# Where the input matrices of a state space are formed: on the states' partitions, or on the channels' partitions

## The chip, the cores and the metric

The kernel runs on one core of a Trainium2 chip. The metric is device time in microseconds (us), the median of several executions. It was 3431.4 us in 3 runs of the kernel before (3431.08 to 3432.77).

## The reference

The model is a stack of four layers on 512 tokens of width 2048, all in float32. The first layer holds gated linear attention (GLA) and forgetting attention, the second a diagonal state space (S5), and the last two other mixtures. Only the state space matters here:

```python
# 128 groups of 16 channels, each with a 64-dim complex diagonal state
step = exp(log_step); mag = exp(lr * step)
lb = mag * (cos(li * step) + 1j * sin(li * step))      # the power of one token
coef = (lb - 1) / (lr + 1j * li)
bb = coef[..., None] * b                                # scaled B: state x channel
x_t = lb * x_{t-1} + bb @ u_t
y_t = real(c @ x_t) + d * u_t
```

The kernel works it in blocks of `ST` = 8 tokens. For a block it needs, for each pair of groups, a matrix that takes 8 tokens of 16 channels (128 rows, token e and channel c) to the 128 states of the pair. Its entry is the scaled B of the channel times the power 7 - e of lb. These "B tables" do not depend on x, so they are made early and stored in DRAM.

## The kernel before

**Products and helpers.** Nearly all time goes to weight products (line 631). Each float32 product is made of three passes of rounded halves. A weight piece of 512 KB is loaded by SP into a ring of 4 (`load_piece`, line 351), ACT makes its high half (line 390), DVE the low half (line 396), PE then multiplies: 24 matmuls of 512 columns for a usual piece. SP issues the load of piece n+7, ACT and DVE split piece n+3, and PE multiplies piece n, all at the same place of their programs. `load_piece` waits until DVE has split the piece that held the slot.

**Side work.** Each engine runs a generator of side steps woven among its pieces by `beside` and `between` (line 855). For the first phase, `GLA_IN` (41 pieces), the side work is `prep_*` (lines 2061 to 2353). It has 56 steps: a lead of 4, then 8 slices (`SSL`) of 6 steps, called `at` 0 to 5, and 4 last ones. A slice is 8 pairs of groups. About four pieces, 8 half pieces, lie in a slice. No engine keeps time with another except through semaphores; an instruction that waits holds up all that stands behind it on its engine, the pieces too.

**Steps of a slice before.** DVE scales B (`scaled_b`, `at` 0, six instructions of 128 elements), multiplies it by the eight powers (`b_powers`, `at` 1 and 2, twice three instructions of 1024 elements, lines 2292 to 2294) and does the same for C (`c_powers`, `at` 3 and 4, lines 2304 to 2309), then the phases (`at` 5). PE turns the B tables by 16 transposes (`turn_b`, `at` 2 and 3, line 2119), and turns C by 4 (line 2109, `at` 5). In `at` 0 of the next slice it makes 32 small products (`kernels`, line 2130), which need `c_powers` of the slice done. ACT copies the turned B from PSUM to `s_BT` (four copies of 512 columns, line 2170), among other copies. SP stores the phases' table (`s_turns`, `at` 1), loads the next slice's B and C (12 DMAs, lines 2070 and 2075, `at` 2), stores the small products of the slice before (`s_k`, 8 DMAs, line 2096, `at` 3), and stores `s_bt` and `s_c_powers` (line 2078, `at` 5). Slice 0 has no `s_k`.

After the phase POOL waits for all tables and loads the operands of GLA (`gla_pool`, line 969).

Of the kernel before, what the change touches and what calls it, by code (L numbers as in the profile page):

```python
# [127 lines left out]
def build(nc, inp, out):  # L128
# [840 lines left out]
    def gla_pool(pool):  # L969
        wait_stored(pool, GLA_IN)  # L970
        pool.wait_ge(s5_kept, 16 * PREP_TABLES * SSL)
        pool.wait_ge(s5_kept_k, 16 * SPAIR * SSL)
# [1009 lines left out]
    def diff_first(pool):  # L1982
# [34 lines left out]
    V5 = overlay(HALF, [  # L2017
        ("s_b", [2, SPAIR, SC], F32), ("s_B", [2, SPAIR, SC], F32), ("s_BP", [2, SPAIR, 2, SC], F32), ("s_cn", [4, P], F32),
        ("s_c", [2, SPAIR, SC], F32), ("s_C", [2, SPAIR, E9, SC], F32), ("s_tp", [SPAIR, E9, SC], F32),
        ("s_L", [2, SPAIR, ST, SC], F32), ("s_t", [SPAIR, ST, SC], F32), ("s_BT", [2, SPAIR, P], F32), ("s_cs", [3, SPAIR, SK], F32),  # L2020
        ("s_n", [SPAIR, SK], F32), ("s_K", [2, 2 * P], F32), ("s_d", [NPAIR // 4, SC], F32),
        ("s_same", [4 * SC], F32)])
    V6 = overlay(0, [
# [25 lines left out]
    PREP_LOADS, PREP_TABLES = 12, 3  # L2049

    def s5_natural(n):

# [8 lines left out]
    def prep_sp(sp):  # L2061
# [15 lines left out]
        def keep(table, n, sl):  # L2077
            sp.dma_start(table[sl], n).then_inc(s5_kept, 16)

        for step, sl, at in prep_slots():  # L2080
            if step == 0:
                sp.wait_ge(x_stored, 16)
# [10 lines left out]
            if at == 3 and 0 < sl <= SSL:  # L2093
                sp.wait_ge(s5_k, sl)
                for n in range(SPAIR):
                    sp.dma_start(k_dram[sl - 1][:, n, :, :], V5["s_K"][n * SC:(n + 1) * SC, :, :]).then_inc(s5_kept_k, 16)
            if at == 5 and 0 <= sl < SSL:
                sp.wait_ge(s5_bte, 2 * sl + 2)
                keep(bt_dram, V5["s_BT"][:, :, :, :].rearrange("p n j x -> p (n j x)"), sl)
                sp.wait_ge(s5_c, sl + 1)  # L2100
                keep(c_dram, V5["s_C"][:, :, :, :, :].rearrange("p n j e c -> p (n j e c)"), sl)
            yield

    def prep_pe(pe):
        def turn_c(sl):
            pe.wait_ge(s5_in, 16 * PREP_LOADS * (sl + 1))
            pe.wait_ge(s5_bte, 2 * sl)
# [4 lines left out]
        def turn_b(sl, n):  # L2112
            pe.wait_ge(s5_l, 2 * sl + n + 1)
            if n == 0:
                pe.wait_ge(s5_cc, sl + 1)
            else:
                pe.wait_ge(s5_ke, sl)
            for j in range(SPAIR):
                ins = nc.tensor.transpose(pm[2 * n + j // 4][:, j % 4 * P:(j % 4 + 1) * P], V5["s_L"][:, n, j, :, :], ident[:, :])
            ins.then_inc(s5_bt, 1)  # L2120

        def kernels(sl):
            pe.wait_ge(s5_bte, 2 * sl + 2)
            pe.wait_ge(s5_c, sl + 1)
            pe.wait_ge(s5_bp, sl + 1)
            for half_of in range(2):
# [8 lines left out]
        for step, sl, at in prep_slots():  # L2135
            if at == 0 and 0 < sl <= SSL:
                kernels(sl - 1)
            if at in (2, 3) and 0 <= sl < SSL:
                turn_b(sl, at - 2)
            if at == 5 and sl < SSL - 1:  # L2140
                turn_c(sl + 1)
            yield
# [1 line left out]
    def prep_act(act):  # L2144
# [21 lines left out]
        def copy_b(sl, n):  # L2166
            act.wait_ge(s5_bt, 2 * sl + n + 1)
            act.wait_ge(s5_kept, 16 * PREP_TABLES * sl)
            for h in range(2):
                ins = nc.scalar.activation(V5["s_BT"][:, n, 4 * h:4 * h + 4, :], pm[2 * n + h][:, :], ACT.Copy)  # L2170
                run(ins) if h == 0 else ins.then_inc(s5_bte, 1)
# [13 lines left out]
        for step, sl, at in prep_slots():  # L2185
# [18 lines left out]
                copy_kernels(sl - 1)  # L2204
            if at == 1 and 0 <= sl < SSL:
                spread_b(sl)
            if at in (3, 4) and 0 <= sl < SSL:
                copy_b(sl, at - 3)
            yield

    def prep_dve(dve):
# [57 lines left out]
        def scaled_b(sl):  # L2269
# [4 lines left out]
            dve.wait_ge(s5_l, 2 * sl)  # L2274
            for n in range(2):
                run(tt(t[:, :, 0, :], V5["s_b"][:, n, :, :], over_c(S_CR), ALU.mult))
                run(tt(t[:, :, 1, :], V5["s_b"][:, 1 - n, :, :], over_c(S_CI), ALU.mult))
# [1 line left out]
                run(ins) if n == 0 else ins.then_inc(s5_b, 1)  # L2279

        def b_powers(sl, n):
            js = slice(sl * SPAIR, (sl + 1) * SPAIR)
            power = lambda c: ang[:, c, :ST, js].rearrange("p e j -> p j e").unsqueeze(3).broadcast_to([P, SPAIR, ST, SC])
            b3 = lambda x: V5["s_B"][:, x, :, :].unsqueeze(2).broadcast_to([P, SPAIR, ST, SC])
            if n == 0:
                dve.wait_ge(s5_b, sl + 1)
                dve.wait_ge(s5_sc, 3)
            else:
                dve.wait_ge(s5_l, 2 * sl + 1)
            if sl:  # L2290
                dve.wait_ge(s5_bt, 2 * (sl - 1) + n + 1)
            run(tt(V5["s_L"][:, n, :, :, :], b3(n), power(0), ALU.mult))
            run(tt(t[:, :, :, :], b3(1 - n), power(1), ALU.mult))
            tt(V5["s_L"][:, n, :, :, :], V5["s_L"][:, n, :, :, :], t[:, :, :, :], ALU.subtract if n == 0 else ALU.add).then_inc(s5_l, 1)

        def c_powers(sl, n):
            js = slice(sl * SPAIR, (sl + 1) * SPAIR)
# [24 lines left out]
        for step, sl, at in prep_slots():  # L2322
# [22 lines left out]

    def prep_pool(pool):
# [12 lines left out]
    def s5_sp(sp):  # L2359
# [40 lines left out]
    def s5_pe(pe):  # L2400
        for sl in range(SSL):
# [4 lines left out]
            ins.then_inc(s5_ut, 1)  # L2406
            yield
            pe.wait_ge(s5_ute, sl + 1)
            pe.wait_ge(s5_bt_in, 16 * (sl + 1))
            pe.wait_ge(s5_ze, 2 * sl)  # L2410
            for n in range(2):
                for g in range(NG):
# [71 lines left out]
    def s5_dve(dve):  # L2484
# [353 lines left out]
```

## Time and profile before

| | |
|---|---|
| median of 3 runs | 3431.4 us |
| profiled execution | 3432.28 us |
| its span | 3430.5 us |
| PE busy in the span | 3341.5 us (97%) |
| DVE busy | 1638.5 us (48%) |
| ACT busy | 1291.4 us (38%) |
| mean granted clock | 0.991 |
| share of 16 DMA engines of the main hardware queue | 33.0% |

The span is counted from the first to the last instruction. The clock is that which TensorE was granted, as a part of full speed. Busy shares are means over stages of different make; the stage that the change touches lies between about 57 and 310 us. SP computes nothing, so the table has no row for it: its time is that of issuing DMAs and of waiting.

### The profile page before, as it was taken

The numbers are of one execution on the slowest core, as the hardware profiler recorded it, in microseconds if no ns is written. First come the engines' busy times: TensorE is split into PE (matmuls) and PEld (weight loads), VectorE is DVE, ScalarE is ACT, GpSimd is POOL, SyncE is SP. The second block draws the span as 40 slices with busy tenths as digits, with TensorE's granted clock in tenths as the row PEclk, the third lists the DMA queues.
The fourth block names the chain that finished last, engine by engine and source line by source line (L and its number), as shares of the span: only waits on it lengthen the run. The fifth ranks groups of instructions, "written<-read, shape, count | busy, mean of one in ns | idle before, by whom it ended". The sixth has DMA issues, their size and how long they took to land.

```text
span 3430.5 us, 41764 instructions
## 1 busy us (share of the span) xinstructions
PE 3341.5 (97%) x16431; PEld 2700.0 (79%) x16431; DVE 1638.5 (48%) x2695; ACT 1291.4 (38%) x2000; POOL 515.0 (15%) x749
## 2 busy tenths in 40 slices
PE   7999999999999999999999899999999999999998
PEld 6777887887888888888888676788878888777886
DVE  7895655344343454444343556553424343355443
ACT  4443433343233333433342436532323323355432
POOL 0001312322110000110330011021000111110211
PEclk9999999999999999999999999999999999999999
DMA  6776433546348776544335343363433643433642
GB/s 211 216 231 199 132 105 105 154 145 208 132 160 227 210 215 184 173 159 141 123 111 170 119 129 102 122 214 119 147 88 111 200 151 117 132 111 102 208 148 92
DMA packets 279523, 525.06 MB, mean 153 GB/s; under 512 B 64189, under 2 KB 99588, under 8 KB 274720
## 3 DMA queue, kind: packets, MB, share of 16 engines
q1 hardware_dynamic: 223504, 340.79, 33.0%
q0 software_dynamic: 53648, 178.32, 15.2%
q10 hardware_dynamic: 2176, 3.28, 0.4%
q8 instruction: 131, 2.15, 0.3%
q14 instruction: 64, 0.52, 0.0%
HBM read 408.32 MB, written 113.97 MB: 152 GB/s over the span
## 4 chain that ended last, share of the span: by engine, by line
PE 73%; DVE 3%; ACT 3%; issue 2%; DMA 1%; POOL 0%; ACTq 0%; POOLq 0%; DVEq 0%
PE pg L631 64%; PE pm L1322 2%; PE pm L1351 2%; PE pm L1338 1%; PE pm L2426 1%; ACT whi L390 1%; DMA mx_g<-zt 1%; PE pm L2430 0%; PE pm L2414 0%; DVE r_y L1707 0%; DVE d_x L2514 0%; PE pm L2405 0%; ACT stage L501 0%; PE pm L1819 0%; ACT w_p L1387 0%
## 5 line engine op out<-in xcount | busy, mean ns | idle before, releaser
L396 DVE TENSOR_TENSOR wlo<-raw,whi 128x1024 fp32r<-128x1024 f32 x523 | 663.2, 1273 | 1251.5 <-ACT whi L390 1250.5
L390 ACT ACTIVATE whi<-raw 128x1024 fp32r<-128x1024 f32 x523 | 548.7, 1054 | 1100.3 <-PE pg L631 1090.2
L631 PE MATMUL pg<-a_hi,whi 128*128 128x512 f32 x1856 | 743.9, 401 | 11.4 <-DVE wlo L396 4.8
L631 PE MATMUL pg<-a_hi,wlo 128*128 128x512 f32 x1856 | 726.7, 392 | 0.0
L631 PE MATMUL pg<-a_lo,whi 128*128 128x512 f32 x1856 | 726.2, 391 | 0.0
L631 PE MATMUL pg<-b_hi,whi 128*128 128x512 f32 x1568 | 620.8, 396 | 8.7 <-DVE stage L572 3.2
L631 PE MATMUL pg<-b_hi,wlo 128*128 128x512 f32 x1568 | 612.2, 390 | 0.0
L631 PE MATMUL pg<-b_lo,whi 128*128 128x512 f32 x1568 | 611.5, 390 | 0.0
L631 PEld LDWEIGHTS pg<-a_hi,whi 128*128 128x128 f32 x1856 | 348.4, 188 | 90.7 <-issue 14.2
L631 PEld LDWEIGHTS pg<-a_hi,wlo 128*128 128x128 f32 x1856 | 348.1, 188 | 77.5
L631 PEld LDWEIGHTS pg<-a_lo,whi 128*128 128x128 f32 x1856 | 348.7, 188 | 73.6 <-issue 2.6
L631 PEld LDWEIGHTS pg<-b_hi,whi 128*128 128x128 f32 x1568 | 295.3, 188 | 73.9 <-issue 6.4
L631 PEld LDWEIGHTS pg<-b_hi,wlo 128*128 128x128 f32 x1568 | 294.9, 188 | 62.5
L631 PEld LDWEIGHTS pg<-b_lo,whi 128*128 128x128 f32 x1568 | 295.3, 188 | 60.8 <-issue 1.2
L673 POOL DMA_DIRECT2D zt<-stage x144 | 78.1, 545 | 569.6 <-DVE stage L572 290.3
L631 PE MATMUL pg<-whi,a_hi 128*128 128x512 f32 x384 | 156.5, 407 | 0.0
L631 PE MATMUL pg<-wlo,a_hi 128*128 128x512 f32 x384 | 150.8, 393 | 0.0
L631 PE MATMUL pg<-whi,a_lo 128*128 128x512 f32 x384 | 150.4, 392 | 0.0
L1387 ACT ACTIVATE m_p<-m_p,m_small 128x128 f32<-128x128 f32 (+3 forms) x96 | 54.1, 563 | 211.0 <-DVE m_small L1453 210.6
L1450 DVE CUSTOM_DVE_ANT_0 m_p<-pm,wide 128x128 f32<-128x128 f32 (+3 forms) x96 | 47.1, 491 | 138.7 <-PE pm L1322 69.5
L685 POOL TENSOR_TENSOR acc<-acc,xa_sq 128x512 f32<-128x512 f32 x44 | 60.9, 1384 | 314.0 <-ACT xa_sq L525 309.1
L631 PE MATMUL pg<-whi,b_hi 128*128 128x512 f32 x256 | 101.7, 397 | 0.0
(442 smaller groups left out, 3843.7 us busy)
## 6 DMA issues: line engine op xcount, KB each, us to landing
raw<-in_l_w_in SPq DMA_DIRECT2D x169, 512.0 KB, 3.7
raw<-in_ab_w_in SPq DMA_DIRECT2D x112, 512.0 KB, 3.7
zt<-stage POOLq DMA_DIRECT2D x142, 256.0 KB, 3.6
raw<-in_c_w_in SPq DMA_DIRECT2D x64, 512.0 KB, 4.9
raw<-in_l_w_out SPq DMA_DIRECT2D x64, 512.0 KB, 3.9
raw<-in_ab_w_out SPq DMA_DIRECT2D x32, 512.0 KB, 3.8
raw<-in_glu_w SPq DMA_DIRECT2D x32, 512.0 KB, 4.2
raw<-in_c_w_out SPq DMA_DIRECT2D x32, 512.0 KB, 3.7
```

The source lines that it names most:

```text
L390: nc.scalar.activation(used(whi, n), used(raw, n), ACT.Copy).then_inc(hi_ready, 1)
L396: nc.vector.tensor_tensor(used(wlo, n), used(raw, n), used(whi, n).bitcast(F32), ALU.subtract).then_inc(lo_ready, 1)
L631: ins = nc.tensor.matmul(pg[m][:r.rows(m), :r.cols()], lhsT, rhs, start=(kt == 0 and n_pass == 0), stop=(kt == r.kts - 1 and n_pass == 2))
L673: pool.dma_start(r.dst(i, m, r), stage[:r.rows(m), m, :r.cols()]).then_inc(stored[m], 16)
L685: nc.gpsimd.tensor_tensor(total[:, :], total[:, :], squares[:, m % 2, :], ALU.add).then_inc(acc_done, 1)
L1322: ins = nc.tensor.matmul(pm[n % 2][:, :count * P], lhsT, rhs, start=(i == 0), stop=(i == len(ops) - 1))
L1338: ins = nc.tensor.transpose(pm[2][:, at:at + P], p[:, b * P:(b + 1) * P], ident[:, :])
L1351: ins = nc.tensor.matmul(pm[3][o * a.dv:(o + 1) * a.dv, qb * P:(qb + 1) * P], a.value(t, o, first + b), a.buf["pt"][:, n % 2, at:at + P], ...
L1387: nc.scalar.activation(p, p, ACT.Exp, bias=a.buf["small"][:, s:s + 1], accum_out=a.buf["small"][:, 4 + s:5 + s]).then_inc(att["probs"], 1)
L1450: run(vec.tensor_tensor_reduce(out=a.buf["p"][:, s, :count * P], in0=pm[n % 2][:, :count * P], in1=a.bias(t, qb, count), scale=a.scale, sc ...
L2426: nc.tensor.matmul(y_of(j), V6["d_x"][:, n, j, :, :].rearrange("p g k -> p (g k)"), V6["d_C"][:, n, j, 1:, :], start=(n == 0 and j % 4 == ...
```

## The change

B tables are now formed with (token, channel) on the partitions. The powers are turned once, by 8 transposes (`turn_powers`), copied by ACT and stored in DRAM as rows. For each slice the scaled B is turned by 2 transposes, copied by one ACT instruction and stored in DRAM (`b_rows`). When this store has landed, SP issues 24 loads (`repeat_rows`), each into 16 partitions, which repeat the rows of B for the eight tokens and each power row for the 16 channels. DVE multiplies the two in the following slice (`b_powers(sl - 1)`, still six instructions of 1024 elements), straight into `s_BT`, and SP stores the table one slice later, too. Semaphores of the later state-space phase are used twice, so its counts are offset.

```diff
+        def repeat_rows(sl):
+            for e in range(ST):
+                rows_of = slice(e * SC, (e + 1) * SC)
+                power = powers_rows[:, e:e + 1, sl * SPAIR:(sl + 1) * SPAIR, :].rearrange("n a j x -> a n (j x)")
+                sp.dma_start(V5["s_Pr"][rows_of, :, :, :].rearrange("p n j x -> p n (j x)"),
+                             power.broadcast_to([SC, 2, SPAIR * P])).then_inc(rows_repeated, 16)
+                for n in range(2):
+                    sp.dma_start(V5["s_Br"][rows_of, n, :, :], b_rows[sl][:, n, :].rearrange("(j c) x -> c j x", c=SC)).then_inc(
+                        rows_repeated, 16)
...
+            if at == 0 and sl == 0:
+                sp.wait_ge(s5_bte, 1)
+                sp.dma_start(powers_rows.rearrange("n (h e) j x -> (e j) (n h) x", e=2), V5["s_BT"][:, 0, :, :]).then_inc(rows_kept, 16)
+            if at == 3 and 0 < sl <= SSL:
+                sp.wait_ge(s5_l, 2 * sl)
+                sp.dma_start(bt_dram[sl - 1], V5["s_BT"][:, :, :, :].rearrange("p n j x -> p (n j x)")).then_inc(b_tables_kept, 16)
+            if at == 3 and 0 <= sl < SSL:
+                sp.wait_ge(s5_bte, sl + 2)
+                sp.dma_start(b_rows[sl], V5["s_bT"][:, :, :]).then_inc(rows_kept, 16)
+            if at == 4 and 0 <= sl < SSL:
+                sp.wait_ge(rows_kept, 16 * (sl + 2))
+                repeat_rows(sl)
             if at == 5 and 0 <= sl < SSL:
-                sp.wait_ge(s5_bte, 2 * sl + 2)
-                keep(bt_dram, V5["s_BT"][:, :, :, :].rearrange("p n j x -> p (n j x)"), sl)
                 sp.wait_ge(s5_c, sl + 1)
                 keep(c_dram, V5["s_C"][:, :, :, :, :].rearrange("p n j e c -> p (n j e c)"), sl)
...
-            for j in range(SPAIR):
-                ins = nc.tensor.transpose(pm[2 * n + j // 4][:, j % 4 * P:(j % 4 + 1) * P], V5["s_L"][:, n, j, :, :], ident[:, :])
+        def turn_powers():
+            pe.wait_ge(s5_sc, 3)
+            for n in range(2):
+                for h in range(ST // 2):
+                    ins = nc.tensor.transpose(pm[1 + 2 * n][:, h * P:(h + 1) * P],
+                                              T5["s_ang"][:, n, 2 * h:2 * h + 2, :].rearrange("p e j -> p (e j)"), ident[:, :])
             ins.then_inc(s5_bt, 1)
+        def turn_b(sl):
+            pe.wait_ge(s5_b, sl + 1)
+            pe.wait_ge(s5_bte, sl + 1)
+            for n in range(2):
+                ins = nc.tensor.transpose(pm[3][:, n * P:(n + 1) * P], V5["s_B"][:, n, :, :].rearrange("p j c -> p (j c)"), ident[:, :])
+            ins.then_inc(s5_bt, 1)
...
+        def copy_b(sl):
+            act.wait_ge(s5_bt, sl + 2)
+            act.wait_ge(rows_kept, 16 * (sl + 1))
+            nc.scalar.activation(V5["s_bT"][:, :, :], pm[3][:, :2 * P], ACT.Copy).then_inc(s5_bte, 1)
...
         def b_powers(sl, n):
...
             if n == 0:
+                dve.wait_ge(rows_repeated, 16 * ROW_LOADS * (sl + 1))
+                dve.wait_ge(rows_kept, 16)
+                dve.wait_ge(b_tables_kept, 16 * sl)
+            to, by, tp = V5["s_BT"][:, n, :, :], V5["s_Pr"], t.rearrange("p j e c -> p j (e c)")
+            run(tt(to, V5["s_Br"][:, n, :, :], by[:, 0, :, :], ALU.mult))
+            run(tt(tp, V5["s_Br"][:, 1 - n, :, :], by[:, 1, :, :], ALU.mult))
+            tt(to, to, tp, ALU.subtract if n == 0 else ALU.add).then_inc(s5_l, 1)
...
-                if at in (1, 2):
-                    b_powers(sl, at - 1)
...
+            if at in (1, 2) and 0 < sl <= SSL:
+                b_powers(sl - 1, at - 1)
```

## Rows read from the trace of the kernel before

**Rows 1.** Windows: length, busy time of each engine, PEclk, DMA share, GB/s.

```profile
80.00:300.00 220.00, 214.28 (x1224) 169.06 (x1223) 190.19 (x215) 92.48 (x156) 15.68 (x25) 1.00 0.74 228
50.00:55.00 5.00, 2.96 (x7) 2.39 (x8) 4.75 (x5) 3.57 (x4) 0.00 (x0) 0.52 0.37 93
```

**Rows 2.** Waits of PE, DVE and SP between 80 and 300 us: total, times, longest.

```profile
PE pm L2119 <- DVE s_L L2294: 5.7, 8, 1.0
...
DVE wlo L396 <- ACT whi L390: 24.5, 13, 6.1
...
SPq L369 <- DVE wlo L396: 79.9, 22, 11.0
SPq L2078 <- DVE s_C L2309: 22.6, 8, 3.1
```

**Rows 3.** Timeline of SP: start, time and count of merged issues; slice 1 to 2.

```profile
126.08 0.47 SPq L2078 DMA_DIRECT2D s_bt<-s_BT  x1
129.23 0.33 SPq L2078 DMA_DIRECT2D s_c_powers<-s_C  x1
132.75 4.75 SPq L369 DMA_DIRECT2D raw<-in_ab_w_in  x2
137.54 1.38 SPq L2078 DMA_DIRECT2D s_turns<-s_cs  x1
...
147.03 0.50 SPq L369 DMA_DIRECT2D raw<-in_ab_w_in  x1
147.57 3.87 SPq L2096 DMA_DIRECT2D s_k<-s_K  x8
151.51 0.40 SPq L369 DMA_DIRECT2D raw<-in_ab_w_in  x1
151.96 0.47 SPq L2078 DMA_DIRECT2D s_bt<-s_BT  x1
```

**Rows 4.** SP's timeline at slice 0's store, and in the later state-space phase.

```profile
99.73 0.46 SPq L2078 DMA_DIRECT2D s_bt<-s_BT  x1
...
1088.27 6.23 SPq L2373 DMA_DIRECT2D d_MG<-s_k  x8
```

**Rows 5.** DMA issues: count, KB each, median us to landing; the last from 1050 to 1350 us.

```profile
s_bt<-s_BT SPq DMA_DIRECT2D x8, 1024.0 KB, 6.4
...
s_k<-s_K SPq DMA_DIRECT2D x64, 32.0 KB, 3.0
s_cn<-in_s_c_re SPq DMA_DIRECT2D x32, 32.0 KB, 1.9
...
d_MG<-s_k SPq DMA_DIRECT2D x64, 128.0 KB, 8.6
```

**Rows 6.** Timeline of DVE in slice 7: first b_powers, its end, and last c_powers.

```profile
269.18 1.28 DVE L2292 TENSOR_TENSOR s_L<-s_B,s_ang 128x1024 f32<-128x1024 f32 x1
...
275.53 1.23 DVE L2294 TENSOR_TENSOR s_L<-s_L,s_t 128x1024 f32<-128x1024 f32 x1
276.68 1.22 DVE L396 TENSOR_TENSOR wlo<-raw,whi 128x1024 fp32r<-128x1024 f32 x1
...
285.91 1.36 DVE L2309 SCALAR_TENSOR_TENSOR s_C<-s_C,s_tp 128x1152 f32<-128x1152 f32 x1
```

**Rows 7.** Timeline of PE at the first eight transposes of a slice, and at `turn_c`.

```profile
219.03 0.39 PE L631 MATMUL pg<-wlo,a_hi 128*128 128x512 f32 x1
220.17 1.10 PE L2119 MATMUL pm<-ident,s_L 128*128 128x128 f32 x8 [0.74 <-DVE s_L L2294]
221.02 0.48 PE L631 MATMUL pg<-whi,a_hi 128*128 128x512 f32 x1
...
232.86 0.40 PE L631 MATMUL pg<-wlo,a_hi 128*128 128x512 f32 x1
233.09 0.60 PE L2109 MATMUL pm<-ident,s_cn 128*128 128x128 f32 x4
233.45 0.47 PE L631 MATMUL pg<-whi,a_hi 128*128 128x512 f32 x1
```

**Rows 8.** Timeline: the last `kernels` on PE, POOL's first GLA load, its user.

```profile
288.77 1.08 PE L2130 MATMUL pm<-s_C,s_BP 128*32 128x128 f32 x32
...
308.70 0.52 POOL L973 DMA_DIRECT2D g_lr<-zt  x1 [3.56 <-DMA zn<-stage]
...
325.36 1.12 PE L1023 MATMUL pm<-g_lr,g_up 16*128 16x512 f32 x2
```

More of the change, by code:

```diff
@@ L971, in gla_pool @@
         pool.wait_ge(s5_kept, 16 * PREP_TABLES * SSL)
+        pool.wait_ge(b_tables_kept, BEFORE_BT)
         pool.wait_ge(s5_kept_k, 16 * SPAIR * SSL)
@@ L2019, in build @@
         ("s_c", [2, SPAIR, SC], F32), ("s_C", [2, SPAIR, E9, SC], F32), ("s_tp", [SPAIR, E9, SC], F32),
-        ("s_L", [2, SPAIR, ST, SC], F32), ("s_t", [SPAIR, ST, SC], F32), ("s_BT", [2, SPAIR, P], F32), ("s_cs", [3, SPAIR, SK], F32),
+        ("s_Br", [2, SPAIR, P], F32), ("s_Pr", [2, SPAIR, P], F32), ("s_bT", [2, P], F32), ("s_t", [SPAIR, ST, SC], F32), ("s_BT", [2, SPAIR, P], F32), ("s_cs", [3, SPAIR, SK], F32),
         ("s_n", [SPAIR, SK], F32), ("s_K", [2, 2 * P], F32), ("s_d", [NPAIR // 4, SC], F32),
@@ L2028, in build @@
     bt_dram, c_dram = dram("s5_bt", (SSL, P, 2 * SPAIR * P)), dram("s5_c_powers", (SSL, P, 2 * SPAIR * E9 * SC))
+    b_rows, powers_rows = dram("s5_b_rows", (SSL, P, 2, P)), dram("s5_powers_rows", (2, ST, NPAIR, P))
     cs_dram, k_dram = dram("s5_turns", (SSL, P, 3 * SPAIR * SK)), dram("s5_k", (SSL, SC, SPAIR, 2, 2 * P))
@@ L2048, in build @@
     PREP_STEPS = PREP_LEAD + PREP_SLOT * SSL + PREP_LAST
-    PREP_LOADS, PREP_TABLES = 12, 3
+    PREP_LOADS, PREP_TABLES = 12, 2
+    ROW_LOADS = 3 * ST
+    b_tables_kept, rows_kept, rows_repeated = s5_bt_in, s5_cs_in, s5_mat_in
+    BEFORE_BT, BEFORE_CS, BEFORE_MAT = 16 * SSL, 16 * (SSL + 1), 16 * ROW_LOADS * SSL
     def s5_natural(n):
@@ L2106, in turn_c @@
             pe.wait_ge(s5_in, 16 * PREP_LOADS * (sl + 1))
-            pe.wait_ge(s5_bte, 2 * sl)
+            pe.wait_ge(s5_cc, sl)
             for i in range(4):
@@ L2110, in turn_c @@
             ins.then_inc(s5_ct, 1)
[L2112 to L2117, printed above, removed]
-            for j in range(SPAIR):
-                ins = nc.tensor.transpose(pm[2 * n + j // 4][:, j % 4 * P:(j % 4 + 1) * P], V5["s_L"][:, n, j, :, :], ident[:, :])
+        def turn_powers():
[10 more added lines that the diff above has]
+                ins = nc.tensor.transpose(pm[3][:, n * P:(n + 1) * P], V5["s_B"][:, n, :, :].rearrange("p j c -> p (j c)"), ident[:, :])
             ins.then_inc(s5_bt, 1)
         def kernels(sl):
-            pe.wait_ge(s5_bte, 2 * sl + 2)
+            pe.wait_ge(s5_ke, sl)
             pe.wait_ge(s5_c, sl + 1)
@@ L2137, in prep_pe @@
                 kernels(sl - 1)
-            if at in (2, 3) and 0 <= sl < SSL:
-                turn_b(sl, at - 2)
+            if at == 0 and sl == 0:
+                turn_powers()
+            if at == 1 and 0 <= sl < SSL:
+                turn_b(sl)
             if at == 5 and sl < SSL - 1:
@@ L2164, in copy_c, with copy_powers @@
                     run(ins) if n + g < 2 else ins.then_inc(s5_cc, 1)
[L2166 to L2171, printed above, removed]
+        def copy_powers():
+            act.wait_ge(s5_bt, 1)
+            for n in range(2):
+                ins = nc.scalar.activation(V5["s_BT"][:, 0, 4 * n:4 * n + 4, :], pm[1 + 2 * n][:, :], ACT.Copy)
+                run(ins) if n == 0 else ins.then_inc(s5_bte, 1)
+        def copy_b(sl):
+            act.wait_ge(s5_bt, sl + 2)
+            act.wait_ge(rows_kept, 16 * (sl + 1))
+            nc.scalar.activation(V5["s_bT"][:, :, :], pm[3][:, :2 * P], ACT.Copy).then_inc(s5_bte, 1)
         def phase_sines(sl):
@@ L2206, in prep_act @@
                 spread_b(sl)
-            if at in (3, 4) and 0 <= sl < SSL:
-                copy_b(sl, at - 3)
+            if at == 0 and sl == 0:
+                copy_powers()
+            if at == 2 and 0 <= sl < SSL:
+                copy_b(sl)
             yield
@@ L2273, in scaled_b @@
             dve.wait_ge(s5_bp, sl)
-            dve.wait_ge(s5_l, 2 * sl)
+            dve.wait_ge(s5_bt, sl + 1)
             for n in range(2):
@@ L2281, in b_powers @@
         def b_powers(sl, n):
-            js = slice(sl * SPAIR, (sl + 1) * SPAIR)
-            power = lambda c: ang[:, c, :ST, js].rearrange("p e j -> p j e").unsqueeze(3).broadcast_to([P, SPAIR, ST, SC])
-            b3 = lambda x: V5["s_B"][:, x, :, :].unsqueeze(2).broadcast_to([P, SPAIR, ST, SC])
             if n == 0:
-                dve.wait_ge(s5_b, sl + 1)
-                dve.wait_ge(s5_sc, 3)
-            else:
-                dve.wait_ge(s5_l, 2 * sl + 1)
[L2290 to L2294, printed above, removed]
+                dve.wait_ge(rows_repeated, 16 * ROW_LOADS * (sl + 1))
[5 more added lines that the diff above has]
+            tt(to, to, tp, ALU.subtract if n == 0 else ALU.add).then_inc(s5_l, 1)
+            if n == 0:
+                dve.wait_ge(s5_l, 2 * sl + 1)
         def c_powers(sl, n):
@@ L2375, in s5_sp @@
         sp.wait_ge(s5_kept, 16 * PREP_TABLES * SSL)
+        sp.wait_ge(b_tables_kept, BEFORE_BT)
         sp.wait_ge(s5_kept_k, 16 * SPAIR * SSL)
@@ L2408, in s5_pe @@
             pe.wait_ge(s5_ute, sl + 1)
-            pe.wait_ge(s5_bt_in, 16 * (sl + 1))
+            pe.wait_ge(s5_bt_in, BEFORE_BT + 16 * (sl + 1))
             pe.wait_ge(s5_ze, 2 * sl)
@@ L2421, in s5_pe @@
             pe.wait_ge(s5_xp, sl + 1)
-            pe.wait_ge(s5_mat_in, 16 * (ST + 1) * (sl + 1))
+            pe.wait_ge(s5_mat_in, BEFORE_MAT + 16 * (ST + 1) * (sl + 1))
             y_of = lambda j: pm[j // 4][:, j % 4 * P:(j % 4 + 1) * P]
@@ L2497, in s5_dve @@
             dve.wait_ge(s5_v, sl + 1)
-            dve.wait_ge(s5_cs_in, 16 * (sl + 1))
+            dve.wait_ge(s5_cs_in, BEFORE_CS + 16 * (sl + 1))
             for n in range(2):
```

## The prediction

> **What bounds the kernel now.** I read the page first (PE busy 97% of the span), then windows, waits and timelines of the stage that the change touches. From 80 to 300 us, which hold nearly all eight slices, PE is busy 214.3 of 220 us and DVE 190.2 [rows 1]. PE bounds, with DVE close behind. PE's only named wait there is for the B powers, 5.7 us, which the change removes; DVE idles 24.5 us for ACT's half, that is for PE's pace [rows 2]. The engine that no busy row shows is SP. In one slice, from one s_bt store to the next (126.08 to 151.96, 25.9 us), it idles 2.7 us before s_c_powers, 3.2 before the weight loads and 4.0 between the two (4.75 less two issues), 9.9 in all. It issues for 16.0 us [rows 3]. Eight s_k stores of only 32 KB take 3.87 us there, and 12 loads of B and C lie in the gap between 138.9 and 147.0: a small DMA costs SP about half a microsecond whatever its size. SP has 10 us a slice to spare; that is the number to hold the change against.
>
> **What goes.** PE: eight transposes hold up the products from 219.03 to 221.02, 1.99 us against a cadence of 0.23 (24 of which make a piece of 5.5 us), so 1.76 us with 0.74 us of waiting; the second eight of a slice I take at the same less the wait, 1.0. So 2.75 us a slice, 22 us in eight [rows 7]. ACT loses four copies and gains one, and it waits elsewhere: nothing on the path. DVE keeps six instructions of the same size. Their operands are no longer broadcast; from below I would take 1.0 us each, from above the 1.28 of the row, and I take no change [rows 6].
>
> **What comes on PE and ACT.** Two transposes a slice: four cost 0.59 - 0.23 = 0.36 us at `turn_c`, so about 0.3, 2.4 us in all, and 0.9 once for the powers [rows 7]. PE's net gain, if it alone decided, is 22 - 3.3 = 19 us. `turn_powers` makes the first `scaled_b` wait a few us; DVE is 3 pieces ahead of PE's need there, so nothing.
>
> **What comes on DMA.** A slice adds 2 MB of loads and 0.13 MB of store to 220 us x 228 GB/s / 8 = 6.3 MB. At 228 GB/s and share 0.74 the engines run at 308 GB/s when busy, so 2.2 MB is 7 us on top of 0.74 x 25.9 = 19 us. With 26 us a slice the engines would be just full [rows 1].
>
> **What comes on SP.** A slice gains 24 loads, each into 16 partitions, and the b_rows store (0.5 us); the s_bt store only moves. The trace has no such load. Nearest in cost from below is the s_k store, 3.87 / 8 = 0.48 us [rows 3]; from above the d_MG load, also rows of 512 B into 16 partitions but twice the size of a B repeat, 6.23 / 8 = 0.78 [rows 4]. I take 0.5, near s_k, because 8 of the 24 have long rows and the other 16 are half of d_MG. So 12 us, with ends 11.5 and 18.7.
>
> Before the loads SP waits until b_rows has landed. It is issued 0.5 us behind the 1 MB s_bt store on the same queue. Bounds: 3.0 us (s_k, small) and 6.4 (s_bt) [rows 5]; I take 6.0, because it stands behind s_bt. A weight issue of 0.4 lies in between, so SP stands still for 5.6. Behind it on SP are the loads and then every weight piece.
>
> SP alone: 16.0 + 0.5 + 12 + 5.6 = 34.1 us a slice, against 25.9.
>
> **The loop through DVE** is a little longer. From the last repeat issued: it lands (1.9 us as s_cn, 8.6 as d_MG [rows 5]; I take 4.0); DVE's b_powers, 269.18 to 276.76, 7.6 us, and the next low half 1.2 [rows 6], for which SP's weight load before `at` 3 waits; this issue 0.4; s_k 3.9; s_bt and b_rows 0.9; b_rows lands 6.0; 24 issues 12. The sum is 36.0 us a slice. SP's own 34.1 hides inside this loop, and so does PE's net work of 25.9 - 2.4 = 23.5. DVE stands at b_powers, with weight halves and c_powers behind it; PE has three split pieces in hand, but its `kernels` need c_powers, which ended at 287.27 with PE there at 288.77: 1.5 us of slack and no more [rows 6, 8]. So PE goes at the loop's pace.
>
> **The sum.** In slice 0 SP reaches its fifth step near 99.7, where it issued s_bt before [rows 4]; b_rows was issued some 11 us earlier, so no wait. Repeats end at 111.7 and land at 115.7. Six loops more: 115.7 + 6 x 36.0 = 331.7, where b_powers(6) starts. At the same place of DVE's program b_powers(7) started at 269.18 before [rows 6]. Delay 62.5; less the slack 1.5, the last `kernels` are 61 us late. The last slice's rows land at 331.7 + 36 = 367.7, DVE is held once more for about 10 us, of which PE's reserve (some 20 us of pieces) covers all but about 2: 63. POOL's first GLA load at 308.70 now waits for the last s_bt, which lands about 11 us later than these 61; its user on PE starts at 325.36, 16 us behind [rows 8], and covers that. So 3432.3 of the profiled execution + 63 = 3495.3; the median of the runs is 0.9 lower: **3494 us**.
>
> PE stands about 12 us in each loop. After a standstill near 47 us its granted clock was 0.52 for five us [rows 1], the 1.2 GHz level against 2.4. Half speed for 5 us costs about 2.5 us a loop, and PE has 12 to spare. I take nothing.
>
> The Trainium skill, page "DMA: Bandwidth & Descriptors", section "Issuing engines are not separate DMA queues", calls the sequencer time to start a DMA usually small relative to the DMA itself. By it the 24 loads would cost their transfer, about 7 us instead of 12, a loop of 31 and 3464 us. The s_k row speaks against it: 8 issues are 3.87 us for a quarter of a megabyte. It stays in the range as its lower part.
>
> **Rivals.**
> (a) Faster, about 3415: SP's added work hides in its 9.9 us and in DVE's distance, and PE's 19 us are had, up to DVE's spare 24.5 less its share outside the slices (about 2 us a slice, 16 in all), since DVE is at 24 of 26 us. Place: `turn_b` on PE. For it: PE is the busiest engine now. Against: the loop would have to be under 26 us, with the 24 issues and the b_rows landing under 8 us together where I have 18. 3432.3 - 17 = 3415.
> (b) Mildly slower, about 3448: the store lands before SP is there and DVE's wait is covered, so only the issues count, 16.0 + 0.5 + 12 = 28.5 a slice: 115.7 + 6 x 28.5 = 286.7, 17.5 late, less 1.5. For it: landings are often hidden. Against: SP does nothing between the store and the wait but one weight issue.
> (c) Much slower, about 3573: the repeats find the DMA engines full, issues cost 0.78 and land in 8.6 as d_MG. Loop 36 + 6.7 + 4.6 = 47.3: first landing 127, + 6 x 47.3 = 410.8, 142 late. With issues at 0.78 alone: loop 42.7, 109 late, 3541. For it: engines at 0.74 already. Against: a longer loop leaves the engines 26 of 36 us.
> (d) No change: gain of (a) eaten by about as much waiting, a loop of 26. Nothing in particular supports it.
>
> **How the numbers follow.** Forecast 0.68, (a) 0.08, (b) 0.10, (c) 0.11, (d) 0.03. Faster by over 0.2% (7 us, about what can be told here) 0.08, within 0.03, slower 0.89. The range: from below a loop of 31 to 32 (short landings of both kinds, 3 + 2 us, or cheap issues) gives +29 to +35; from above issues at 0.65 alone give a loop of 39.6 and +88, a landing of 6 alone 38 and +77, both +102: 3460 to 3535, between the one and the both.
>
> **What would show it.** SP's timeline: 24 issues in a run of about 12 us a slice, with SP idle 5 to 6 us before them. DVE waiting at its first product of b_powers, about 10 us a slice, seven times or so, released by DMA; PE waiting at line 2130's counterpart for c_powers about as long, and some stretches at the lower clock. The period of the s_c_powers stores 36 us instead of 26. The transposes 24 instead of 128. Wrong if the period stays under 28 us, or if the repeats are issued at 0.3 us each, or if PE does not wait in this stage. The rest of the kernel should be unchanged within 3 us.

## The result, and the profile after

The changed kernel takes 3542.1 us (median of 4 runs, 3540.96 to 3546.86) against 3431.2 us for the kernel before on the same chip: 1.0327 times as long [1.031, 1.0343], 110.8 us more. The forecast was 3494. The direction was right, the size was not, and the time lies outside the range, by 7 us.

The page of the changed kernel: span, PE's row, the clock in 40 slices of 88 us, and the main hardware queue.

```profile
span 3539.7 us, 41713 instructions
...
PE 3342.9 (94%) x16327; PEld 2700.4 (76%) x16327; DVE 1634.1 (46%) x2695; ACT 1277.0 (36%) x1978; POOL 517.0 (15%) x749
...
PEclk9878899999999999999999999999999999999999
...
q1 hardware_dynamic: 247200, 359.15, 36.3%
```

PE is busy for 3342.9 us where it was 3341.5: the 104 transposes that went are not seen, because the clock is lower in the stage of the change (slices 2 to 5 of the clock row) and each matmul takes longer there. All that was added is standstill. Windows of the same 220 us as [rows 1], and of the 120 after them:

```profile
80.00:300.00 220.00, 150.74 (x765) 116.72 (x764) 128.53 (x146) 54.69 (x94) 11.15 (x18) 0.84 0.93 200
300.00:420.00 120.00, 82.37 (x423) 66.15 (x422) 67.32 (x74) 29.48 (x47) 6.94 (x11) 0.86 0.92 210
```

Before, PE was busy in 214.3 of the 220 us, and the DMA engines in 0.74 of the time while they moved 228 GB/s. Now PE has 150.7, and the DMA engines are busy in 0.93 of the time for only 200 GB/s. They work more and move less: that is the first thing to explain. The waits between 60 and 440 us, which hold all slices (total, times, longest; SP's idle gaps are in the last two):

```profile
DVE s_BT L2326 <- DMA s_Br<-s_b_rows: 117.5, 8, 16.9
...
PE pm L2135 <- DMA s_cn<-in_s_c_im: 82.6, 6, 16.5
...
PE pm L2161 <- issue: 21.0, 5, 18.3
...
PE pm L1024 <- DMA g_masks<-in_masks: 3.5, 1, 3.5
...
SPq L369 <- DVE wlo L396: 44.0, 7, 16.0
SPq L2090 <- DMA s_b_rows<-s_bT: 20.6, 7, 3.0
```

DVE waits for the repeats, as forecast. PE however stands at the transposes of C (L2135), whose loads SP issues behind the repeats, and not mainly at `kernels`. SP, which idled 9.9 us a slice before [rows 3], has its only regular gap where it waits for `b_rows` to land, 3.0 us each; the 44.0 us for DVE lie ahead of the first repeats and behind the last loads of B and C. One slice of SP's timeline, from repeat to repeat:

```profile
138.59 0.33 SPq L2090 DMA_DIRECT2D s_Pr<-s_powers_rows  x1
...
151.30 0.51 SPq L2083 DMA_DIRECT2D s_c_powers<-s_C  x1
...
153.49 8.25 SPq L2075 DMA_DIRECT2D s_b<-in_s_b_re  x2
161.78 4.22 SPq L2075 DMA_DIRECT2D s_b<-in_s_b_im  x2
166.04 3.72 SPq L2080 DMA_DIRECT2D s_cn<-in_s_c_re  x4
169.81 1.85 SPq L2080 DMA_DIRECT2D s_cn<-in_s_c_im  x4
171.71 0.43 SPq L369 DMA_DIRECT2D raw<-in_ab_w_in  x1
172.19 4.06 SPq L2112 DMA_DIRECT2D s_k<-s_K  x8
...
181.08 0.33 SPq L2090 DMA_DIRECT2D s_Pr<-s_powers_rows  x1
```

The slice lasts 42.5 us here (41.7 in the mean of six). The 24 repeats are issued in 12.7 us, a little over half a microsecond each, as forecast. What was not: the 12 loads of B and C behind them, unchanged by the diff, hold SP from 153.49 to 171.66, 18.2 us where they took 8.0 before. Landings between 60 and 440 us (count, KB each, median us):

```profile
...
s_Pr<-s_powers_rows SPq DMA_DIRECT2D x64, 128.0 KB, 6.5
s_Br<-s_b_rows SPq DMA_DIRECT2D x128, 64.0 KB, 6.8
...
s_b_rows<-s_bT SPq DMA_DIRECT2D x8, 128.0 KB, 4.3
```

DVE's first product of slice 1, and of the slice that I forecast at 331.7:

```profile
161.56 1.23 DVE L2326 TENSOR_TENSOR s_BT<-s_Br,s_Pr 128x1024 f32<-128x1024 f32 x1 [16.90 <-DMA s_Br<-s_b_rows]
...
369.00 1.22 DVE L2326 TENSOR_TENSOR s_BT<-s_Br,s_Pr 128x1024 f32<-128x1024 f32 x1 [15.69 <-DMA s_Br<-s_b_rows]
```

The repeats of this slice went out from 138.59 to 151.25; the last landed at 161.5, 23 us after the first was issued and 10 after the last. And the lines that answer to [rows 8], the last `kernels`, POOL's first GLA load, and its user on PE:

```profile
387.13 1.94 PE L2161 MATMUL pm<-s_C,s_BP 128*32 128x128 f32 x32 [18.27 <-issue]
```

```profile
426.40 0.52 POOL L974 DMA_DIRECT2D g_lr<-zt  x1 [21.40 <-DMA s_bt<-s_BT]
...
433.33 1.12 PE L1024 MATMUL pm<-g_lr,g_up 16*128 16x512 f32 x2 [3.54 <-DMA g_masks<-in_masks]
```

They are 98.4, 117.7 and 108.0 us later than before. The spans differ by 109.2: all of it arises in this stage, and the rest of the kernel adds 1.

### The profile page after: what moved, and what is told of

Read it like the earlier page. It is cut to its first block, busy times and chain, and to the rows that moved or that the text cites. A ratio compares the mean times of both kernels' runs of the same rounds, so it can differ in the third digit from the quotient of the medians.

```text
span 3539.7 us, 41713 instructions
## 1 busy us (share of the span) xinstructions
PE 3342.9 (94%) x16327; PEld 2700.4 (76%) x16327; DVE 1634.1 (46%) x2695; ACT 1277.0 (36%) x1978; POOL 517.0 (15%) x749
## 4 chain that ended last, share of the span: by engine, by line
PE 70%; DVE 3%; ACT 3%; DMA 2%; issue 2%; POOL 0%; ACTq 0%; POOLq 0%; DVEq 0%
PE pg L631 61%; PE pm L1323 2%; PE pm L1352 2%; DMA mx_g<-zt 1%; PE pm L1339 1%; PE pm L2463 1%; ACT whi L390 1%; PE pm L2467 0%; PE pm L2451 0%; DVE r_y L1708 0%; DVE d_x L2551 0%; ACT stage L501 0%; PE pm L2442 0%; ACT w_p L1388 0%; PE pm L1820 0%
```

## The experiments

Eleven kernels ran. Each is compared with the kernel before on the same chip (3429.8, 3433.0 or 3431.4 us). `e8`, `e10` and `e11` change the kernel before, the others the changed kernel.

**Three ways to make the repeats cheaper for the DMA engines.** My theory at this point: the transfers of the repeats, not their issues, make the 6 us a slice that the forecast lacks. First, an eighth of the bytes in the same 24 loads (DVE zeroes the two buffers once):

```diff
-                sp.dma_start(V5["s_Pr"][rows_of, :, :, :]..., power.broadcast_to([SC, 2, SPAIR * P]))
+                sp.dma_start(V5["s_Pr"][rows_of, :, 0, :], power[:, :, :P].broadcast_to([SC, 2, P]))
...
-                    sp.dma_start(V5["s_Br"][rows_of, n, :, :], b_rows[sl][:, n, :].rearrange("(j c) x -> c j x", c=SC))
+                    sp.dma_start(V5["s_Br"][rows_of, n, 0, :], b_rows[sl][:SC, n, :])
```

> The 24 repeat loads of a slice are issued as in the changed kernel and waited for as there, but each moves an eighth of its bytes (0.25 MB a slice instead of 2), so the B tables are incomplete. Two memsets of DVE are added once (about 2.5 us). Theory A (the repeats' transfer is what I mis-sized: the DMA engines drain 2 MB in some 20 us, and SP's small loads queue behind them): the 12 loads of B and C take 8 us of SP again instead of 18, the rows land within 3 us, the slice falls from 41.8 to SP's own sum 16.0 + 0.5 + 12 + 4 = 32 to 33 us; about 9 x 7 = 60 us less than the changed kernel, near 3478. Theory B (it is the count of issues and SP's waits alone): the slice stays near 41 us and the time near 3540.

3497.4 us, 1.0197 [1.0168, 1.0227]. From one `s_c_powers` store to the next are 35.9 us: with an eighth of the bytes the stage has the period that I had forecast with all of them. Its SP timeline at the loads of B and C:

```profile
186.11 1.39 SPq L2075 DMA_DIRECT2D s_b<-in_s_b_re  x2
187.55 3.46 SPq L2075 DMA_DIRECT2D s_b<-in_s_b_im  x2
191.05 3.94 SPq L2080 DMA_DIRECT2D s_cn<-in_s_c_re  x4
195.03 1.85 SPq L2080 DMA_DIRECT2D s_cn<-in_s_c_im  x4
```

The loads of B and C take 10.8 us and not 18.2. So 43 us of the 111 (68 stay) hang on the bytes of the repeats. Next the same bytes into other partitions: token e of channel c goes to partition 8c + e instead of 16e + c (a table in another order of rows; what reads it later is not adapted).

```diff
-                rows_of = slice(e * SC, (e + 1) * SC)
+                rows_of = slice(e, P, ST)
```

> Each repeat load writes the 16 partitions e, e+8, e+16, ... instead of 16 neighbours; bytes, packets, sources and issues are the same, the rows of the B tables are in another order. 
3523.7 us, 1.0274 [1.0244, 1.0304]. Its window and a landing:

```profile
80.00:300.00 220.00, 158.25 (x827) 122.75 (x826) 137.73 (x161) 58.02 (x101) 11.16 (x18) 0.85 0.70 210
```

```profile
s_Br<-s_b_rows SPq DMA_DIRECT2D x128, 64.0 KB, 2.4
```

The same bytes land in 2.4 us instead of 6.8, and the engines' share falls from 0.93 to 0.70 while they move more. The loads of B and C are back at 10.9 us. The Trainium skill, page "SBUF — State Buffer", section "Door 1: The DMA port swizzle", says that the rate of a DMA depends on how many of the 16 ports its partitions reach, and that a narrow band of neighbours reaches few. The trace agrees, 6.8 against 2.4 us. But the loss fell by only 17 us, to 94. Each issue got dearer, 0.60 us instead of 0.43 to 0.47, and the 24 take 16.3 us instead of 12.7 (12.3 in `e1`):

```profile
217.61 0.58 SPq L2090 DMA_DIRECT2D s_Pr<-s_powers_rows  x1
218.23 1.24 SPq L2093 DMA_DIRECT2D s_Br<-s_b_rows  x2
```

Those 4.0 us are what separates the mean slice of `e2` from that of `e1`, 39.2 against 35.3 us: once the rows are apart, the bytes cost nothing more that can be seen.

The third: the power loads read 16 different rows of DRAM instead of one row 16 times (values that are not the powers).

```diff
-                             power.broadcast_to([SC, 2, SPAIR * P])).then_inc(rows_repeated, 16)
+                             powers_rows.rearrange("n a (s j) x -> (a s) n (j x)", s=SSL)[6 * e:6 * e + SC]).then_inc(rows_repeated, 16)
```

> The power loads read 16 different rows of 4 KB instead of one row 16 times, so the powers in the tables are wrong; destination, bytes and issues are the same. Theory A2 (the same row read by 16 engines is slow): the half of the bytes that is powers gets fast, the slice falls by 5 us or more, time 3505 or less. Theory A1: no change, 3540 (within 5).

3538.9 us, 1.0318 [1.0288, 1.0348]; the loads land in 6.3 us. Reading one row many times costs nothing that can be seen beside the slow writes. What is narrow is where the repeats are written.

**The order on SP.** The loads of B and C go ahead of the repeats:

```diff
-            if at == 2 and 0 <= sl < SSL - 1:
-                load(sl + 1)
...
+                if sl < SSL - 1:
+                    load(sl + 1)
                 sp.wait_ge(rows_kept, 16 * (sl + 2))
                 repeat_rows(sl)
```

> The 12 loads of the next slice's B and C are issued right after the b_rows store, ahead of the repeats instead of behind them; everything else as in the changed kernel. Theory A: they take 8 us of SP instead of 18, hide the 3 us wait for b_rows; SP's slice would be about 42 - 10 - 3 = 29, but the repeats still drain for 20 us, so that DVE's b_powers end the loop: first repeat to landing 21 + products and half 9 + s_k, stores 5 + loads 8 = 43 less what the loads hide. So between 36 and 43 us a slice, 3500 to 3545, no big gain because the drain stands in the loop anyway. Theory B (SP's occupation alone): 29 to 31 us, near 3465.

3552.3 us, 1.0357 [1.0327, 1.0387]. Its SP timeline:

```profile
200.35 0.79 SPq L2083 DMA_DIRECT2D s_turns<-s_cs  x1
218.08 0.37 SPq L369 DMA_DIRECT2D raw<-in_ab_w_in  x1
...
223.23 2.25 SPq L2075 DMA_DIRECT2D s_b<-in_s_b_re  x2
...
228.98 1.86 SPq L2080 DMA_DIRECT2D s_cn<-in_s_c_im  x4
```

In this place the 12 loads take 7.6 us again: their 18.2 us are the backlog that stands ahead of them. But nothing is won, the slice is 43.9 us. SP now stands 16.9 us (201.1 to 218.1) before a weight load that needs DVE, and DVE is held by the same repeats. The drain of the repeats is either in SP's issues or in DVE's wait; moving it between them does not take it away. This is the loop through DVE of the forecast, now as the bound, with a landing far over 4.0.

**Everything but the repeats.** No repeats, no wait for them; DVE multiplies zeros.

```diff
-            if at == 4 and 0 <= sl < SSL:
-                sp.wait_ge(rows_kept, 16 * (sl + 2))
-                repeat_rows(sl)
...
-                dve.wait_ge(rows_repeated, 16 * ROW_LOADS * (sl + 1))
```

> The changed kernel without the 24 repeat loads and without the wait for the b_rows store; DVE makes the same products from tiles zeroed once, so the B tables hold zeros. All else of the change stays (fewer transposes and copies, the row stores). Theory: everything the change loses comes from the repeats; what is left is PE's gain, capped by DVE's spare time of about 2 us a slice: 8 x 2 = 16 us less than before, between 3413 and 3422. Rival (the move of b_powers by a slice, or the waits between DVE, PE and ACT in slice 0, cost something themselves): 3430 or more.

3427.2 us (10 runs) against 3433.0, 0.9986 [0.9976, 0.9995]. The whole cost is the repeats, with the wait ahead of them; all the rest of the change is worth 6 us, not the 19 of PE that I counted, and less than I expected of this run too (3413 to 3422). The stores of `s_c_powers` are 25.9 us apart, as before. PE waits 9.4 us at `kernels` between 60 and 400 us, and is busy for 209.6 of the 220 us.

**Another engine issues.** POOL issues the row stores and the repeats, with a wait for DVE before them:

```diff
-                sp.wait_ge(rows_kept, 16 * (sl + 2))
-                repeat_rows(sl)
...
+                pool.wait_ge(rows_kept, 16 * (sl + 2))
+                pool.wait_ge(s5_l, 2 * sl)
+                repeat_rows(sl)
```

> The row stores, the wait for them and the 24 repeats are issued by POOL instead of SP; destinations, bytes and order are the same. POOL's queue is another ring of the same 16 DMA engines. Theory (the repeats cost through SP's queue: its issue time, its wait and the backlog ahead of its small loads and weights): SP is as before and its slice sum is 16 us, the drain of 20 us a slice stays, and DVE waits for it: issue 24 x 0.55 = 13, drain to about 20, b_rows 5, so loop 20 + 5 + products 9 = 34 us at most, if POOL's steps are late less hidden; time 3470 to 3500. Rival (the engines' drain alone decides: share 0.93 of 41.8 us): near 3540 still.

3499.0 us, 1.0191 [1.0176, 1.0207]. 45 us of the 111 come back, and 66 stay although SP issues nothing new. Its window:

```profile
80.00:300.00 220.00, 173.31 (x876) 134.73 (x875) 140.08 (x163) 64.76 (x113) 93.11 (x175) 0.87 0.93 228
```

The engines are still 0.93 busy, a repeat now lands in 9.0 us and a weight half in 12.8. And the loads of B and C are still slow to issue (SP's timeline; these are the first 4 loads of 12, and all 12 take 16.8 us):

```profile
185.77 6.62 SPq L2076 DMA_DIRECT2D s_b<-in_s_b_re  x2
192.43 4.36 SPq L2076 DMA_DIRECT2D s_b<-in_s_b_im  x2
```

No repeat is in SP's queue here. So what holds them up is not only what SP itself issued ahead of them: the same narrow writes do it from POOL's queue. If the repeats cost only the time of their issues on SP, nothing would be left. How much of the 66 us is the narrow writes, and how much something else, the last run below tells.

**Fewer issues of the same bytes.** The two B loads of a token in one:

```diff
-                for n in range(2):
-                    sp.dma_start(V5["s_Br"][rows_of, n, :, :], b_rows[sl][:, n, :].rearrange("(j c) x -> c j x", c=SC))
+                sp.dma_start(V5["s_Br"][rows_of, :, :, :], b_rows[sl].rearrange("(j c) n x -> c n j x", c=SC))
```

> The two B loads of a token are one of 128 KB, so 16 issues a slice instead of 24 with the same bytes and packets. If SP's issue count is what holds the loop, it saves 8 x 0.47 = 3.8 us a slice, 7 times: 26 us, near 3515. If the drain of 2 MB into 16 neighbouring partitions decides, SP only meets the backlog sooner (its loads of B and C are blocked longer by as much): 3535 to 3542.

3547.5 us, 1.0334 [1.0313, 1.0355]: no gain. An issue takes 0.56 to 0.60 us instead of 0.43 to 0.47, so 16 take 11.0 us where 24 took 12.7, and the loads behind them again take 18.3. With the engines full the drain decides, not the issues.

**Issues alone, in the kernel before.** 24 loads of 8 KB into a buffer that nobody reads, where the repeats would be:

```diff
+            if at == 4 and 0 <= sl < SSL:
+                sp.wait_ge(s5_mat_in, 16 * 24 * sl)
+                for e in range(ST):
+                    for n in range(3):
+                        sp.dma_start(V5["s_X"][e * SC:(e + 1) * SC, n, :], inp["s5_b_re"][0, :SC]...[:, n * P:(n + 1) * P])
```

> The kernel before, with 24 loads a slice of 8 KB each (512 B into each of 16 partitions) issued by SP at the step where the change issues its repeats; nothing reads them and nothing waits for their data but SP itself, one slice later. Theory: SP has 9.9 us a slice to spare and they cost 24 x 0.47 = 11.3, so a slice grows from 25.9 to 27.3 or 28 (some of the spare lies where it can't be used): 8 to 17 us in all, 3440 to 3448. Rival (weights late behind 11 us of issues use up the ring's reserve each time): 3460 or more. Rival (issues alone are harmless): 3431.

3490.3 us, 1.0166 [1.0149, 1.0183], far over what I expected. Its SP timeline of one slice, which has no gap at all:

```profile
170.62 12.87 SPq L2101 DMA_DIRECT2D s_X<-in_s_b_re  x24
183.54 0.41 SPq L2078 DMA_DIRECT2D s_bt<-s_BT  x1
...
184.47 2.27 SPq L369 DMA_DIRECT2D raw<-in_ab_w_in  x2
...
188.19 1.97 SPq L2070 DMA_DIRECT2D s_b<-in_s_b_re  x2
190.20 4.29 SPq L2070 DMA_DIRECT2D s_b<-in_s_b_im  x2
...
204.95 1.39 SPq L2101 DMA_DIRECT2D s_X<-in_s_b_re  x3
```

The slice is 34.3 us, and SP's own. 16.0 + 12.9 would be 29. The rest: the 3.9 MB of `s_bt`, `s_c_powers`, two weight halves and `s_turns` leave SP within 5 us, right ahead of the loads of B and C, which take 12.0 us for 8.0. Before, SP's gaps kept them apart. So the 9.9 us of idle time that I counted as spare were not all spare: they were in part the time in which a backlog drained.

**Half as many, and the same number spread out.** 12 such loads (against `e8`), and 24 in groups of 6, 9 and 9: ahead of the two stores of `at` 5, behind them, and at `at` 0:

```diff
-                for e in range(ST):
+                for e in range(4):
```

```diff
+            if at == 5 and 0 <= sl < SSL:
+                sp.wait_ge(s5_mat_in, 16 * 24 * sl)
+                extra(0, 6)
...
+                extra(6, 15)
+            if at == 0 and 0 < sl <= SSL:
+                extra(15, 24)
```

> As e8_before_issues, with 12 extra loads a slice instead of 24, at the same step. Theory (SP's spare time is mostly lost when an issue run pushes its later DMAs together, so that the small loads of B and C stand behind s_bt, s_c_powers and two weight pieces): even 12 issues, 5.7 us against 9.9 spare, lengthen the slice to about 28 us: 3440 to 3452. Rival (a plain sum of issue times against the spare): 22 of 26 us, no loss, 3433.

> The 24 extra loads of e8_before_issues, but in three groups of 6, 9 and 9, put where SP of the kernel before stood still (ahead of s_c_powers and of the two weight loads after it). Same count, same bytes. Theory (position and bunching): DMAs keep their distance, the loads of B and C take 8 to 9 us again, the slice is 27 to 29 us, time 3440 to 3458, at least 30 us less than e8. Rival (the count alone): 3490 as e8.

12 loads: 3443.4 us, 1.0038 [1.0027, 1.005], as expected, with a slice of 27.7 us. 24 spread out: 3466.3, 1.0103 [1.0088, 1.0118], which loses 35 us where the single run lost 57, with the same loads. I had expected at least 30 to come back, and it was 22. The loads of B and C take 8.3 us again, and the standstill moved in part into the second group:

```profile
164.79 0.43 SPq L2083 DMA_DIRECT2D s_c_powers<-s_C  x1
165.27 7.50 SPq L2080 DMA_DIRECT2D s_X<-in_s_b_re  x9
...
173.29 4.47 SPq L2080 DMA_DIRECT2D s_X<-in_s_b_re  x9
```

Nine loads of 8 KB take 7.5 us behind two stores of 1 MB and 1.1 MB, and 4.5 a little later.

**Both remedies.** POOL issues, and the rows go to partitions 8 apart; the later phase is put into the same order, so that nothing is left out.

```diff
-                rows_of = slice(e * SC, (e + 1) * SC)
+                rows_of = slice(e, P, ST)
...
-                sp.dma_start(V6["d_MG"][i * SC:(i + 1) * SC, :, :], k[:, :, P - i * SC:2 * P - i * SC])
+                sp.dma_start(V6["d_MG"][i:P:ST, :, :], k[:, :, P - i * SC:2 * P - i * SC])
```

> Both suspects at once: POOL issues the row stores and the repeats as in e6_pool, and each repeat writes 16 partitions at a distance of 8 as in e2_spread. The later phase's copy of u and its loads of the output matrices follow the new order of rows (channel, token), so that nothing is left out. Theory (two separate costs, SP's queue and the transfer into 16 neighbours): POOL's 24 issues of about 0.55 take 13 us, land within 3, then 7.6 of products; loop about 25 with a wait for the products before the next repeats, so near the 26 us of before. Time 3425 to 3445. Rival (the DMA engines or POOL's own issue for such partitions bind in another way): 3470 or more.

3464.8 us, 1.0097 [1.0081, 1.0112]. Two thirds of the loss are gone, but it misses the 3445 that I gave as the most. Its POOL, and its DVE at the same place of two slices:

```profile
188.42 0.52 POOL L2369 DMA_DIRECT2D s_Pr<-s_powers_rows  x1 [12.41 <-DVE s_BT L2309]
...
217.70 0.52 POOL L2369 DMA_DIRECT2D s_Pr<-s_powers_rows  x1 [0.53 <-issue]
```

```profile
180.36 1.23 DVE L2307 TENSOR_TENSOR s_BT<-s_Br,s_Pr 128x1024 f32<-128x1024 f32 x1 [5.53 <-DMA s_Br<-s_b_rows]
...
209.51 1.23 DVE L2307 TENSOR_TENSOR s_BT<-s_Br,s_Pr 128x1024 f32<-128x1024 f32 x1 [2.66 <-DMA s_Br<-s_b_rows]
```

POOL waits for DVE to free the one buffer of repeats and DVE waits for POOL's loads. In the slice shown POOL issues for 12.5 us, the products start 8.6 us later (at 209.51) and take 7.5, and POOL's next issue follows 0.7 behind: 29.3 us, which is the whole slice (217.70 - 188.42). The mean slice is 31.1. Of the 66 us that `e6` left, the distance took away 33, the share of the narrow writes. The 33 that stay I put down to this circle, by the slice shown; a second buffer might open it, but that was not tried. No kernel that does the whole work beat the one before, and by `e5` there are about 6 us to win in this arrangement (at most 8 by its interval).

The periods put the runs in one order. Between the first and the last of the eight `s_c_powers` stores lie seven slices, of 26.3 us in the mean before. So the stage should cost 7 x (mean slice - 26.3):

| | mean slice, us | 7 x (slice - 26.3) | measured over before, us |
|---|---|---|---|
| e5, no repeats | 26.0 | -2 | -6 |
| e10, 12 small issues | 27.7 | 10 | +12 |
| e11, 24 small, spread | 30.9 | 32 | +35 |
| e9, POOL and apart | 31.1 | 34 | +33 |
| e8, 24 small, in a run | 34.3 | 56 | +57 |
| e1, an eighth of the bytes | 35.3 | 63 | +68 |
| e6, POOL issues | 35.6 | 65 | +66 |
| e2, partitions apart | 39.2 | 90 | +94 |
| e3, 16 rows of DRAM | 41.0 | 103 | +109 |
| the change | 41.4 | 106 | +111 |
| e7, 16 issues | 41.8 | 108 | +115 |
| e4, B and C first | 43.6 | 121 | +123 |

No run is off by more than 7 us; what is left lies ahead of the first of these stores or behind the last, in the hand-over to GLA.

## Why the prediction was right in direction and wrong in size

**What bounds it: right.** SP was the engine to hold the change against, though its busy time stands in no row of the page. `e8` shows it without anything else: issues of 8 KB alone cost 57 us.

**What goes, what comes on PE: sized too large.** 19 us of PE net were counted in rival (a). `e5` has 6 [1.7 to 8 by its interval]. DVE's products cost 1.23 us, so there was no change there, as forecast.

**The step that failed: "What comes on DMA".** I had the 2.2 MB go at the stage's mean rate, "7 us on top of 19", and called the engines "just full" at 26 us, with room in any longer loop. Per slice the engines were in fact busy 0.93 x 41.7 = 38.8 us, against 19.2 before: the change adds 19.6 us and not 7. The rate at which the engines ran when busy fell from 308 GB/s to 200 / 0.93 = 215. In `e2` the same bytes give 0.70 x 39.2 = 27.4, 8.3 us more than before: there the 7 would have been nearly right. So the term was mis-sized by the partitions that the loads write to. While they drain, five microseconds look like this (window, PE's busy time, its clock, DMA share, GB/s; a share of about 1 or more in so short a window means full):

```profile
142.00:147.00 5.00, 5.00 (x24) 1.00 1.16 106
157.00:162.00 5.00, 0.00 (x0) 0.97 1.08 358
162.00:167.00 5.00, 0.00 (x0) 0.50 1.02 410
```

Full engines at 106 GB/s with narrow loads, and at 410 GB/s with the others: the stores and weights that had queued up, while SP was still stuck in the loads of B and C. The row that could have warned me stood in my own list: `d_MG`, rows of 512 B into 16 partitions, lands in 8.6 us [rows 5]. I used it as an upper end for one landing, and not for the rate. The drain from the first issue is 23 us, where I had 12 + 4.0 = 16.

**And from it "What comes on SP": 16.0 us held constant.** "SP alone: 34.1": 24 issues 12 (measured 12.7), stands for `b_rows` 5.6 (3.0: it landed in 4.3 though it stands behind a store of 1 MB), and SP's former issues 16.0. The last rose by 10.2 for the loads of B and C. 34.1 + 0.7 - 2.6 + 10.2 = 42.4, and the slice shown lasts 42.5 (41.7 in the mean). An issue is no constant: it depends on what the DMA engines still have to do, in `e6` even for another queue. So SP's own chain sets the loop. "The loop through DVE is a little longer" (36.0) is not what decided: in the slice shown the products end at 169.1, the low half that SP's next weight load needs at 170.2, and SP goes from the last load of C (171.66) to that load without a wait. But that is a margin of 1.4 us only: both chains hold the same drain, and in `e4`, with the loads of B and C ahead of the repeats, DVE is the bound, at 43.9.

**The sum.** First landing 115.7 forecast, 118.8 measured; then six loops of 36.0, measured (369.0 - 118.8) / 6 = 41.7. That is 3.1 + 34.2 = 37.3 us, and `kernels` are 98.4 late and not 61. The upper end of my range, 3535, was the +102 of both terms together and not, as I wrote, a value below it; the time lies above even that.

**The tail: sized too small.** "Covers all but about 2", and the GLA load about 11 us later than the delay, "covers that". Measured, that load is 117.7 - 98.4 = 19.3 us later than the delay, since the last repeats and `s_bt` are slow too, and its user also needs `g_masks`, which is issued 1 us behind and lands in 5.9. From `kernels` to that user PE falls back by 108.0 - 98.4 = 9.6 us: 6.1 of two waits, and some 4 of a clock of 0.92 over 48 us. So 37.3 + 9.6 - 2 = 44.9 of the 46.2 that separate 63 from 109.2, and 1.2 more arise behind that user.

**The clock: "I take nothing".** PE stands up to 18 us at a time, and in the second of two windows in which it does nothing (above) the granted clock is 0.50, the 1.2 GHz level. Inside the loop SP's chain has no term of PE, so I take it that it cost nothing there, as said, though no run separates it; the 4 us of the tail are the exception.

**The rivals.** (a), (b) and (d) fall with the period of 41.7. DVE's "24 of 26 us" in (a) is 22.4 by its row (190.2 of 220 us) [rows 1]; even without repeats PE's gain did not come (`e5`). (c) said "the repeats find the DMA engines full", which is what happened, and has a landing of 8.6 for the 6.8 measured. But it put the price into dearer issues, 0.78 each, where the trace has 0.53. The number of its variant with dearer issues alone, 3541, is right for a wrong reason, by luck: 10.2 us of the loop lie in loads that the change does not touch. The reason I gave against (c), that a longer loop leaves the engines 26 of 36 us, is the failed step again.

The other time, 3464, came from the Trainium skill, page "DMA: Bandwidth & Descriptors", section "Issuing engines are not separate DMA queues", which calls the time to start a DMA usually small relative to the DMA. For one DMA the trace agrees: a repeat takes 0.53 us to issue and 6.8 to land. The price that I drew from it does not follow, since issues come one after the other: `e8` adds 0.2 MB a slice, and costs 57 us.

## What to carry to other kernels

Before a DMA is sized by bytes over the mean rate, look in the trace for a load of the same shape on the on-chip side: how many partitions, how far apart. And when an issuing queue gets a burst of work, do not add its issues to the old ones: issues that stand behind a backlog take longer, even when another engine issued the backlog, and idle gaps of that queue may be what kept them short.

## What the hardware did that I had not expected

- 16 neighbouring partitions against 16 at a distance of 8, same bytes: 6.8 and 2.4 us to land, DMA share 0.93 and 0.70. The price of the distance is the issue: 24 take 16.3 us on SP and not 12.7. On POOL the 24 take 12.5 us with either. There the distance gains less: 9.0 and 6.5 us to land (`e6`, `e9`).
- SP takes 8.25 us to issue two loads of 32 KB each behind the backlog of the repeats, 6.6 when POOL issued the repeats (`e6`), and 1.4 with an eighth of their bytes (`e1`). It is not the bytes of the load itself.
- A store of 128 KB issued 0.5 us behind one of 1 MB takes 4.3 us to land, about as long as that one (4.2).
- Reading one DRAM row into 16 partitions is as fast as reading 16 rows, in this backlog (`s_Pr` 6.5 and 6.3 us); alone it was not measured.
